# A ring of eight weight slots instead of six in a one-layer hybrid decoder with 32 experts

## The reference, cut to what matters

```python
h = rmsnorm(x, norm_mix); q_b, k_b, v_b, z_u, z_v, q_c, gate_logits = split(h @ w_in)
a_out = chunk_spatial_gate(gelu(z_u), layernorm(gelu(z_v)), w_spatial, b_spatial)
b_out = combined dilated window attention (3 head groups of 4 heads of 64)
c_out = cross attention into 256 memory tokens (4 heads of 128)
x = x + (sig(g_A) * (a_out @ w_branch_a) + sig(g_B) * (b_out @ w_branch_b) + sig(g_C) * (c_out @ w_branch_c)) @ w_out
# MoE, top 4 of 32 experts
logits = rmsnorm(x, norm_ffn) @ w_router + b_router; top 4, softmax over them
gate, up = split(xb @ w_gate_up[e] + b_gate_up[e])      # (1024, 2048) per expert
act = min(gate, 7) * sigmoid(1.702 * min(gate, 7)) * (clip(up, -7, 7) + 1)
y_e = act @ w_down[e] + b_down[e]                       # (1024, 1024) per expert
y = rmsnorm(x + gated sum of y_e, norm_final)
```

## Time and profile before

| | us |
|---|---|
| median of 3 runs | 1391.59 |
| lowest, highest | 1388.70, 1393.43 |
| the profiled execution | 1389.35 |
| its span | 1387.5 |

### The profile page before, as it was taken

The page is one execution under the profiler, slowest core; times in us unless marked ns, Lnnn a source line. Parts: engine busy times, 40 slices in busy tenths (PEclk is TensorE's granted clock), DMA queues, the critical chain, the costliest instruction groups (busy, mean ns, idle before and its releaser), DMA issues.

```text
span 1387.5 us, 19046 instructions
## 1 busy us (share of the span) xinstructions
PE 1315.1 (95%) x7749; PEld 631.3 (45%) x7749; DVE 371.6 (27%) x832; ACT 247.1 (18%) x402; POOL 60.7 (4%) x103
## 2 busy tenths in 40 slices
PE   6999968999996999999999999999999999999997
PEld 5766447768743334333433334333343333343333
DVE  3001685221325222122212222122222122221223
ACT  2010212220223111111211111111121111111112
POOL 2032222200000000000000000000000000000000
PEclk9999979999998999999999999999999999999999
DMA  9999576469954999999999999999999999999993
GB/s 337 380 369 341 199 262 232 137 220 349 354 251 149 397 427 429 427 428 430 427 427 430 428 427 429 430 428 427 430 427 427 430 428 428 429 429 428 427 429 162
DMA packets 56971, 515.13 MB, mean 371 GB/s; under 512 B 5411, under 2 KB 6523, under 8 KB 31568
## 3 DMA queue, kind: packets, MB, share of 16 engines
q1 hardware_dynamic: 50000, 493.68, 86.5%
q0 software_dynamic: 6608, 20.25, 4.5%
q10 hardware_dynamic: 336, 0.82, 0.2%
HBM read 511.21 MB, written 47.52 MB: 403 GB/s over the span
## 4 chain that ended last, share of the span: by engine, by line
PE 57%; DMA 35%; DVE 6%; issue 1%; ACT 1%; SPq 0%; DVEq 0%; ACTq 0%
PE psum L576 55%; DMA weights<-in_w_gate_up 34%; PE psum L579 2%; DMA weights<-in_w_mem_kv 1%; DVE qk L1395 1%; DVE weights L1097 1%; DVE samp L1101 0%; DVE weights L1093 0%; DVE samp L1095 0%; DVE pair L1241 0%; DVE x L1423 0%; ACT th L1560 0%; DVE kvt L1287 0%; DVE kc L1300 0%; DVE bn L1108 0%
## 5 line engine op out<-in xcount | busy, mean ns | idle before, releaser
L576 PE MATMUL psum<-weights,spatial 128*64 128x512 f32 x2048 | 487.5, 602 | 12.6 <-DMA weights<-in_w_gate_up 11.1
L576 PE MATMUL psum<-weights,merged 128*64 128x512 f32 (+2 forms) x1152 | 272.8, 595 | 1.5 <-issue 1.5
L576 PEld LDWEIGHTS psum<-weights,spatial 128*64 128x64 f32 x2048 | 129.3, 136 | 255.8 <-issue 202.8
L1366 DVE TENSOR_TENSOR hT<-psum,hT 128x264 f32<-128x264 f32 x256 | 98.8, 428 | 514.1 <-PE psum L576 514.1
L576 PE MATMUL psum<-hT,weights 128*128 128x264 f32 x704 | 164.7, 391 | 1.2 <-DVE pair L1241 0.9
L576 PEld LDWEIGHTS psum<-weights,merged 128*64 128x64 f32 (+2 forms) x1152 | 89.6, 140 | 156.3 <-issue 154.6
L576 PEld LDWEIGHTS psum<-hT,weights 128*128 128x128 f32 x704 | 133.4, 191 | 28.8 <-DVE pair L1241 4.5
L1622 ACT COPY bT<-psum 128x264 f32<-128x264 f32 x33 | 12.5, 380 | 476.6 <-PE psum L579 476.6
L576 PE MATMUL psum<-bT,merged 64*128 64x264 f32 x512 | 91.6, 435 | 0.0
L1395 DVE TENSOR_SCALAR qk<-psum,lowest 128x512 f32<-128x512 f32 x64 | 48.0, 751 | 158.3 <-PE psum L576 154.8
L576 PEld LDWEIGHTS psum<-bT,merged 64*128 64x128 f32 x512 | 38.5, 184 | 103.8 <-issue 103.8
(11 more groups left out here) (277 smaller groups left out, 723.3 us busy)
## 6 DMA issues: line engine op xcount, KB each, us to landing
weights<-in_w_gate_up SPq DMA_DIRECT2D x128, 2048.0 KB, 24.6
weights<-in_w_down SPq DMA_DIRECT2D x64, 2048.0 KB, 22.9
out<-in_cache_win_kv SPq DMA_DIRECT2D x8, 4094.0 KB, 24.1
weights<-in_w_in SPq DMA_DIRECT2D x13, 2048.0 KB, 13.7
out<-in_cache_win_kv SPq DMA_DIRECT2D x2, 4088.0 KB, 19.5
weights<-in_cache_mem_kv POOLq DMA_DIRECT2D x10, 512.0 KB, 6.4
weights<-in_cache_win_kv POOLq DMA_DIRECT2D x36, 128.0 KB, 4.8
weights<-in_w_mem_kv SPq DMA_DIRECT2D x2, 2048.0 KB, 17.8
```

The lines of the kernel that those rows point to most:

```text
L576: return nc.tensor.matmul(out, lhsT, rhs, start=start, stop=stop, **kw)
L1366: V.tensor_tensor(acc[:, c, :], p_a[j % 2][part], acc[:, c, :], ALU.add).then_inc(s_acc, 1)
```

## The change

- The ring has eight slots (`RING = CHUNKS + 2`), and the slot is no longer fixed by the transfer's place in its expert: transfer number c, counted over all experts, goes to slot c % 8. Slots 0 to 5 are the old six in the order in which they come free in the mixer; slot 6 lies over `memory` (the former `kc` and `qcT`), slot 7 over `late` (the former `qk`, `pair`, the second `th` buffer and the router's weights `wr`), which are allocated as one buffer each.
- Transfers 6 and 7 (the first two of expert 1) are issued before the loops: 6 after the sixth count of `s_xq` and the second `woz`, 7 after the router's product and the third count of `s_xlo`. From transfer 8 on, each waits for the use of the transfer eight places before it.
- 24 transfers are four experts and three turns of the ring, so SyncE's and TensorE's loops run over groups of four experts, with the four written out in the body. SyncE's first group stands ahead of its loop. TensorE's count for a slot's semaphore becomes three turns of the ring per group.
- `h_tok` moves to `spatial`, next to `xg`, which moves to its first 512 columns. `gfin` and the junk output of the last squares move to slots 0 and 1; `gfin` is no longer loaded by ScalarE at step `top` but by SyncE, behind the last weight transfer.
- The loops of VectorE and ScalarE stay as they are.

```diff
+RING = CHUNKS + 2
+UNROLL = 4
-        def chunk_slot(k):
-
-            return k if k < 2 else 2 + (k - 1) % 4
-        qk = sb("qk", [P, 12, NT])
+        late = sb("late", [P, 14 * NT + NT + KD * E])
+        qk = late[:, 0:12 * NT].rearrange("p (a t) -> p a t", a=12)
-        qcT = sb("qcT", [P, CH, NT])
+        memory = sb("memory", [P, CH * NM + 2 * 1024 + CH * NT])
+        qcT = memory[:, CH * NM + 2 * 1024:].rearrange("p (h t) -> p h t", h=CH)
-        kc = sb("kc", [P, CH * NM + 2 * 1024])
+        kc = memory[:, 0:CH * NM + 2 * 1024]
-        h_tok = flat_qk[:, 0:D]
+        h_tok = spatial[:, 512:512 + D]
-        gfin = qcT[:, :, :].rearrange("p a b -> p (a b)")[:, 0:D]
+        slots = [weights_at[:, n * SLOT:(n + 1) * SLOT] for n in (0, 1, 3, 4, 5, 2)] + [memory[:, 0:SLOT], late[:, 0:SLOT]]
+        gfin, square_junk = slots[0][:, 0:D], slots[1].rearrange("p (t c) -> p t c", c=D)
...
+            def wait_used(n32, k):
+
+                if k < GU - 1 or k == GU:
+                    sp.wait_ge(s_used, n32 * USED + min(k + 1, USED))
+                elif k == GU - 1:
+                    sp.wait_ge(s_gu, n32 * 2 + 2)
+                else:
+                    sp.wait_ge(s_y, n32 + 1)
+
+            def experts(n32, e, first=0):
+
+                for c in range(first, UNROLL * CHUNKS):
+                    wait_used(n32 + (c - RING) // CHUNKS, (c - RING) % CHUNKS)
+                    chunk(e + c // CHUNKS, c % CHUNKS, c % RING)
+
+            for c in range(RING):
+                if c < 2:
                     sp.wait_ge(s_mixed, 2 * (CH + HPG))
                     taken(sp, "svct", 1)
+                elif c < CHUNKS:
+                    sp.wait_ge(s_job, last_job[{2: 17, 3: 18, 4: 19, 5: 20}[c]])
+                elif c == CHUNKS:
+                    sp.wait_ge(s_job, job[("woz", 1)] + 1)
+                    sp.wait_ge(s_xq, 6)
                 else:
+                    sp.wait_ge(s_job, job[("rt",)] + 1)
+                    sp.wait_ge(s_xlo, 3)
+                chunk(c // CHUNKS, c % CHUNKS, c)
+            experts(0, 0, RING)
+            with sp.Fori(1, E // UNROLL) as i:
+                experts(i * UNROLL, i * UNROLL)
...
+            wait_used(E - 2, GU)
+            sp.dma_start(gfin, I["norm_final"].rearrange("(a d) -> a d", a=1).to_broadcast([P, D])).then_inc(s_gfin_in, 16)
...
-                with pe.Fori(0, E) as i:
-                    n33 = b * (E + 1) + i
-                    n32 = b * E + i
+                with pe.Fori(0, E // UNROLL) as i:
+                    for u in range(UNROLL):
+                        n33 = b * (E + 1) + i * UNROLL + u
+                        n32 = b * E + i * UNROLL + u
+                        turn_of_ring = (b * (E // UNROLL) + i) * (UNROLL * CHUNKS // RING)
...
+                            c = u * CHUNKS + k // 2
+                            if k % 2 == 0:
+                                pe.wait_ge(s_chunk_in[c % RING], turn_of_ring * 16 + (c // RING + 1) * 16)
...
-                    act.dma_start(gfin, I["norm_final"].rearrange("(a d) -> a d", a=1).to_broadcast([P, D])).then_inc(s_gfin_in, 16)
```

More of the change, by code:

```diff
@@ L259, in build @@
         selh = va[0:REL_BUCKETS + 1, :, :].rearrange("p t c -> p (t c)")[:, 0:NG * HANK].rearrange("p (g x) -> p g x", g=NG)
-        pair = sb("pair", [P, 2 * NT])
+        pair = late[:, 12 * NT:14 * NT]
         sels = pair[0:REL_BUCKETS, 0:(NG + 1) * P].rearrange("p (g x) -> p g x", g=NG + 1)
@@ L283, in build @@
         vself = sb("vself", [P, 2, NS])
-        th = [sb(f"th{n}", [P, NT]) for n in range(2)]
+        th = [sb("th0", [P, NT]), late[:, 14 * NT:15 * NT]]
         tmp = [pair[:, n * NT:(n + 1) * NT] for n in range(2)]
-        wr = sb("wr", [P, KD, E])
+        wr = late[:, 15 * NT:15 * NT + KD * E].rearrange("p (k e) -> p k e", k=KD)
         br = sb("br", [P, E])
-        flat_qk = qk[:, :, :].rearrange("p a b -> p (a b)")
+        flat_qk = late[:, 0:12 * NT]
         xr = flat_qk[:, 0:3 * D].rearrange("p (t c) -> p t c", t=3)
-        h_tok = flat_qk[:, 0:D]
+        h_tok = spatial[:, 512:512 + D]
         rowsT = hT
@@ L305, in build @@
         sel_b = bT_all[:, 744:808].bitcast(BF16)
-        xg = wsp.rearrange("p a b -> p (a b)").rearrange("p (k s) -> p k s", k=KD)
+        xg = spatial[:, 0:512].rearrange("p (k s) -> p k s", k=KD)
         y_tok = flat[:, 0:512]
@@ L348, in build @@
         s_block_in = [sem(f"block_in{n}") for n in range(4)]
-        s_chunk_in = [sem(f"chunk_in{n}") for n in range(CHUNKS)]
+        s_chunk_in = [sem(f"chunk_in{n}") for n in range(RING)]
         s_used = sem("chunks_used")
@@ L427, in _, with chunk @@
                 shift(*c)
[L429 to L439, removed]
+            def chunk(e, k, at):
+                if isinstance(e, int):
+                    if k < GU:
+                        src = I["w_gate_up"][0, e, k * 2 * P:(k + 1) * 2 * P, :].rearrange("(p j) c -> p (j c)", p=P)
+                    else:
+                        src = I["w_down"][0, e, (k - GU) * 4 * P:(k - GU + 1) * 4 * P, :].rearrange("(p j) c -> p (j c)", p=P)
+                elif k < GU:
                     src = I["w_gate_up"][0, bass.ds(e, 1), k * 2 * P:(k + 1) * 2 * P, :].rearrange("e (p j) c -> p (e j c)", p=P)
@@ L442, in chunk_dyn @@
                     src = I["w_down"][0, bass.ds(e, 1), (k - GU) * 4 * P:(k - GU + 1) * 4 * P, :].rearrange("e (p j) c -> p (e j c)", p=P)
-                sp.dma_start(chunk_view(k), src).then_inc(s_chunk_in[s], 16)
-            for k in range(CHUNKS):
-                if k < 2:
+                sp.dma_start(slots[at], src).then_inc(s_chunk_in[at], 16)
+            def wait_used(n32, k):
[3 more added lines that the diff above has]
+                    sp.wait_ge(s_gu, n32 * 2 + 2)
+                else:
+                    sp.wait_ge(s_y, n32 + 1)
[5 more added lines that the diff above has]
+                if c < 2:
                     sp.wait_ge(s_mixed, 2 * (CH + HPG))
                     taken(sp, "svct", 1)
-                else:
[L451 to L468, removed]
+                elif c < CHUNKS:
[3 more added lines that the diff above has]
+                    sp.wait_ge(s_xq, 6)
+                else:
+                    sp.wait_ge(s_job, job[("rt",)] + 1)
[4 more added lines that the diff above has]
+                experts(i * UNROLL, i * UNROLL)
             sp.wait_ge(s_done["posm"], 1)
@@ L472, in _ @@
                 with sp.Fori(1, PASSES) as ps:
-                    with sp.Fori(0, E) as e:
-                        one_expert(ps * E + e, e)
+                    with sp.Fori(0, E // UNROLL) as i:
+                        experts(ps * E + i * UNROLL, i * UNROLL)
+                wait_used(PASSES * E - 2, GU)
+            wait_used(E - 2, GU)
+            sp.dma_start(gfin, I["norm_final"].rearrange("(a d) -> a d", a=1).to_broadcast([P, D])).then_inc(s_gfin_in, 16)
             sp.wait_ge(s_fin, 1)
@@ L899, in one_pass @@
                         pe.wait_ge(s_taken[n % 3], n // 3 + 1)
-                with pe.Fori(0, E) as i:
-                    n33 = b * (E + 1) + i
-                    n32 = b * E + i
[L904 to L912, removed]
-                            if k == KD - 1:
[L914 to L949, removed]
@@ new lines, in one_pass @@
+                with pe.Fori(0, E // UNROLL) as i:
[3 more added lines that the diff above has]
+                        turn_of_ring = (b * (E // UNROLL) + i) * (UNROLL * CHUNKS // RING)
+                        for k in range(KD):
+                            if k == 0:
+                                pe.wait_ge(s_xf, n33 + 1)
+                            c = u * CHUNKS + k // 2
+                            if k % 2 == 0:
+                                pe.wait_ge(s_chunk_in[c % RING], turn_of_ring * 16 + (c // RING + 1) * 16)
+                            w = slots[c % RING][:, (k % 2) * 2 * D:(k % 2 + 1) * 2 * D]
+                            for n in range(2):
+                                last = column_pair(p_h[:, n * 512:(n + 1) * 512], xg[:, k, :], w[:, n * 512:(n + 1) * 512],
+                                                   w[:, D + n * 512:D + (n + 1) * 512], k == 0, k == KD - 1)
+                                if k == KD - 1:
+                                    last.then_inc(s_gu, 1)
+                            if k % 2 == 1 and k < KD - 1:
+                                last.then_inc(s_used, 1)
+                            if k == 1:
+                                pe.wait_ge(s_ytok, n32 + 1)
+                                pe.wait_ge(s_gT, n32 + 1)
+                            if 1 <= k <= PAIRED:
+                                scatter(n32, k - 1)
+                            if k == PAIRED + 1:
+                                pe.wait_ge(s_selb, n32 + 1)
+                                for n in range(2):
+                                    column_pair(p_h[:, n * 512:(n + 1) * 512], sel_b[0:PARTS * E, 0:SLOTS], bias[0:PARTS * E, n * 512:(n + 1) * 512],
```

(26 more changed lines are left out.)

7 lines of the change are left out of this document (2 added, 5 removed).

## The result

| | before | changed |
|---|---|---|
| median us, runs | 1391.10, 4 | 1382.45, 4 |
| lowest, highest | 1388.70, 1393.43 | 1379.97, 1382.81 |
| profiled execution (span) | 1389.35 (1387.5) | 1382.81 (1381.0) |

The ratio is 0.9934, 95% interval 0.9918 to 0.9949: 9.2 us less, between 7.1 and 11.4 (the two medians alone differ by 8.7). The prediction said 9.8.

A forecast was written before the change was run, and what follows sets the result against it. The prediction took the gapless weight stream to bound the kernel's end. Two more slots at 4.89 us each, with unroll and moves at nothing, gave 1391.6 - 9.8 = 1381.8 us, range 1376.5 to 1388.

The forecast's parts named there:

- The stream is the end, at 4.89 us a transfer, whatever its depth: Expert loop: the weight stream fixes the end, 4.89 us per 2 MB transfer, 428 to 429 GB/s at shallow or deep queue.
- depth rival: Expert loop: seven transfers in flight speed the stream until TensorE is the bound, 1372.3 us; chance 0.04.
- Two transfers ahead of the first use bring 9.8 us: Before the expert loops: transfers 6 and 7 no longer wait for expert 0, gaining 2 x 4.89 = 9.8 us.
- one-slot rival: Before the expert loops: transfer 7 comes in late and only one extra slot counts, 1386.7 us; chance 0.07.
- the gap: 436.5 to 448.8 us, all six slots full: engines move 44 GB/s, predicted to go to over 300.
- TensorE alone would bring 19.3 us: Expert loop: upper bound, with TensorE never waiting for the stream no stock can bring more than 19.3 us.
- The turn costs TensorE nothing, four experts' code is held: TensorE's unrolled loop: saved turns bring nothing, and four experts' code (6.8 packets) stays held at no cost.
- the sum: Whole kernel: 9.8 us off for the two slots, nothing for the unroll and other moves, giving 1381.8 us.
- The chain changes over at about 1060 us: Chain of waits: first landing of w_gate_up at about 1060 us instead of 794.
- The code rival: TensorE's loop: a turn's code is not held, seven returns wait for code, 14.3 us slower, 1405.9 us; chance 0.08.
- the bounds: Returns to TensorE's loop head: a code packet costs between about 1.2 us and 4.8 us.
- What else moves costs nothing: Moved buffers, b_down's load and the final gain's load: nothing; uncovered, 1.2 us for the final gain.

The follow-up runs named there:

- stock6: Changed kernel with only six transfers issued before the first chunk is used, each later one waiting for the use six places before: 1392.26 us, ratio 1.0010 to before.
- stock8: The changed kernel unaltered, timed again beside the kernel before on the same chip: 1381.04 us, ratio 0.9931 to before.
- stock8_again: The changed kernel unaltered, timed once more as partner of the version with transfers cut in two: 1381.81 us, ratio 0.9937 to before.
- eight_per_turn: Changed kernel with eight experts written out per loop turn instead of four, whole transfers: 1390.34 us, ratio 0.9995 to before.
- six_plain: Changed kernel put back to six slots and one expert per turn, keeping moved buffers and the last gain's load on SyncE: 1390.92 us, ratio 1.0003 to before.
- half_eight: Changed kernel with eight experts per turn, each expert transfer loading only half its slot (result not the model's): 1373.21 us, ratio 0.9862 to before.

## Why the prediction came out right, point by point

- *The stream is the end, at 4.89 us a transfer, whatever its depth.* Right: 428 to 429 GB/s with the deeper queue too; the issue to landing time of w_gate_up rose from 24.6 to 27.4 us and the rate didn't. The depth rival is out.
- *Two transfers ahead of the first use bring 9.8 us.* Right: 10.0 us of loop length between stock6 and stock8, in two steps of 4.7 and 5.2, and 9.6 us with the landing spread taken off. The one-slot rival is out. The rate in the gap was 266 GB/s, not over 300; the transfers stand partly outside of it. The last of them landed at 450.64 us, 8.9 us behind its issue and not 7.7, and 0.2 us behind the issue of transfer 8. It cost nothing: transfer 8 lands 7.7 us behind its issue (458.08), as transfer 6 did before (456.52).
- *TensorE alone would bring 19.3 us.* Right: 897.28 - 877.91 = 19.4.
- *The turn costs TensorE nothing, four experts' code is held.* Right for TensorE. But "I take yes, at no cost" left out who pays for the first loading: five packets more come while the weights stream (19 to 23 in all, one fewer behind the loop), and a landing can trail by them. By the landing spread that is 1.3 us in the first execution, 0.7 in stock8_again and nothing in stock8, all with 23 packets. This is the one term missing from the sum. With the whole of it the sum is 9.8 - 1.3 = 8.5 us, where the first execution has 897.28 - 888.88 = 8.4; the mean of the three is 9.0.
- *The chain changes over at about 1060 us.* It did at 1013.5, 1068.4 (stock8_again) and 1071.1 us (stock8). The landings in this chain stand two experts (58.7 us) apart, and the predicted time lies within one such step of each.
- *The code rival.* Its mechanism exists, at eight experts per turn, and its price per return was inside the bounds (2.3, 1.9 and 1.8 us; the bounds were 1.2 and 4.8). But the path was named wrongly: the returns stay under TensorE's spare time, and the loss comes through the stream. The size of the code was taken too high as well. In eight_per_turn 51 packets start from 448.6 to 1359.0 us, for 32 experts: 1.6 packets an expert and not 1.7, so 6.4 in a turn of four and 12.8 in a turn of eight. The limit lies between the two; no run shows where. On the Trainium skill's two statements, the trace sides with the 128 KB for TensorE in "Advanced Engine Details and Errata" (ISA Cache): 6.4 packets of 16 KB, some 100 KB, were held and 12.8, some 205 KB, not. The two-block window of the Trainium skill's "Runtime: NRT & Kernel Launch" (Instruction fetch mechanics) would have shown more than 23 packets with four experts per turn.
- *What else moves costs nothing.* Right: six_plain. b_down landed in 6.1 us instead of 2.0 (4.8 taken), with room to spare; the final gain's load stands 29.1 us in the queue instead of 3.4, and nobody waits for it.

## What to carry to other kernels

Where a transfer stream runs without a gap to the end, its end is fixed by how much it has carried when the gapless part begins: look for the last gap before it, and price one more slot as one transfer's time, up to what the other engine alone would take. Code that is written out for such a ring is itself traffic beside the stream, so write out only as much as the ring's period needs. Measure a loop from its own first to its own last piece: that number repeated within 1.3 us where whole times of one kernel scatter by over five, and within 0.1 us once the landing spread was taken off.

## What the runs showed that I had not expected

- 44 more packets of code of 16 KB each cost the weight stream 8.3 us, five times their share of bytes. The rate hardly fell; the last of a transfer's 16 steps came later, 11.7 us behind the first instead of 2.5 to 3.8. The same packets cost nothing where the stream has room (half_eight: 877.92 us, spread 0.80).
- TensorE held the code of four experts (6.4 packets) and reloaded that of eight (12.8) in each turn.
- Cutting 2 MB transfers (16 KB per partition) into 1 MB (8 KB) lowered a saturated stream from 428 to 422 GB/s, also where SyncE had to wait for TensorE in between, and SyncE's issues went from 0.33 to 1.9 us.
